# A two-block transformer kernel on one core: attention fillers reordered, forget sums moved into the key tiles

## What is computed

```
x = x + short_conv_mixer(rmsnorm(x))            # conv
x = x + swiglu(rmsnorm(x))                      # ffn1, hidden 2816
x = x + mla_mixer(rmsnorm(x))                   # mla: 8 heads, causal softmax, 1024x1024 out product
x = x + moe_swiglu(rmsnorm(x))                  # moe: 8 experts, the best 2 per token
h = x + [fox, pool](rmsnorm(x)) @ w_out         # fox: 8 heads of 64, softmax(q.k/8 + c[t] - c[s])
h = h + attention(h, mem) @ w_mem_out           # mem: 4 heads of 128 over 256 memory rows
h = h + swiglu(rmsnorm(h))                      # ffn2
```

## Time and profile before

| | us |
|---|---|
| median of 3 executions | 1348.53 |
| their lowest and highest | 1345.12, 1350.06 |
| profiled execution, own time | 1344.52 |
| its span in the trace | 1342.6 |
| granted TensorE clock (share of full) | 0.998 |

### The profile page before, as it was taken

One profiled execution on the slowest core, in us unless ns is written; L12 is line 12 of the kernel. 1 busy time (PEld: TensorE's weight loads), 2 busy tenths in 40 slices (PEclk: granted clock), 3 DMA queues, 4 the chain that ended last, 5 costly groups with the idle time before them and its releaser, 6 DMA issues.

```text
span 1342.6 us, 16314 instructions
## 1 busy us (share of the span) xinstructions
PE 1295.8 (97%) x6200; PEld 1076.8 (80%) x6200; DVE 929.4 (69%) x902; ACT 832.4 (62%) x902; POOL 39.4 (3%) x51
## 2 busy tenths in 40 slices
PE   8999999998999999999999999999999997999998
PEld 6888888887777788888888888878778776788887
DVE  4776555446759888888888888898876564645542
ACT  5645444346766778787777878777576554644431
POOL 4001000000002000000000000002010000000000
PEclk9999999999999999999999999999999999999999
DMA  9648655544218999999999999999773241455540
GB/s 332 234 152 278 213 188 184 172 124 151 106 63 332 420 359 414 357 410 357 411 351 415 356 411 354 410 365 384 258 283 126 94 158 63 166 187 182 187 157 32
DMA packets 90233, 342.20 MB, mean 255 GB/s; under 512 B 6267, under 2 KB 14160, under 8 KB 66512
## 3 DMA queue, kind: packets, MB, share of 16 engines
q1 hardware_dynamic: 87200, 330.67, 66.0%
q0 software_dynamic: 2816, 10.67, 2.3%
q10 hardware_dynamic: 160, 0.07, 0.0%
HBM read 334.05 MB, written 11.01 MB: 257 GB/s over the span
## 4 chain that ended last, share of the span: by engine, by line
PE 87%; DVE 4%; DMA 3%; ACT 3%; issue 2%; POOL 0%; ACTq 0%; SPq 0%; DVEq 0%
PE bank L1688 27%; PE bank L1690 26%; PE bank L1689 26%; DVE w_lo L367 2%; ACT w_hi L362 1%; DMA moe_slots_in<-h,row_to 1%; DMA raw<-in_moe_w_up 1%; PE bank L2026 1%; DMA raw_beside<-in_moe_w_down 1%; PE bank L1794 1%; PE bank L1821 1%; PE bank L1777 1%; DVE x L1072 1%; PE bank L2019 0%; POOL moe_slots_in L543 0%
## 5 line engine op out<-in xcount | busy, mean ns | idle before, releaser
L367 DVE TENSOR_TENSOR w_lo<-raw,w_hi 128x2048 fp32r<-128x2048 f32 (+3 forms) x246 | 549.1, 2246 | 230.3 <-ACT w_hi L362 229.2
L362 ACT ACTIVATE w_hi<-raw 128x2048 fp32r<-128x2048 f32 (+3 forms) x246 | 460.9, 1883 | 209.9 <-PE bank L1690 197.9
L1688 PE MATMUL bank<-w_hi,xT_hi 128*128 128x512 f32 (+2 forms) x672 | 256.7, 382 | 9.3 <-DVE xT_lo L1130 5.5
L1690 PE MATMUL bank<-w_hi,xT_lo 128*128 128x512 f32 (+2 forms) x672 | 253.4, 377 | 0.0
L1689 PE MATMUL bank<-w_lo,xT_hi 128*128 128x512 f32 (+2 forms) x672 | 253.3, 377 | 0.0
L1688 PE MATMUL bank<-w_hi,gT_hi 128*128 128x512 f32 x512 | 201.7, 394 | 4.7 <-DVE w_lo L367 1.9
L1690 PE MATMUL bank<-w_hi,gT_lo 128*128 128x512 f32 x512 | 200.2, 391 | 0.0
L1689 PE MATMUL bank<-w_lo,gT_hi 128*128 128x512 f32 x512 | 199.8, 390 | 0.0
L1688 PEld LDWEIGHTS bank<-w_hi,xT_hi 128*128 128x128 f32 x672 | 126.8, 189 | 34.6 <-DVE xT_lo L1130 6.8
L367 DVE TENSOR_TENSOR w_lo<-raw_beside,w_hi 128x2048 fp32r<-128x2048 f32 x64 | 145.4, 2290 | 10.0 <-ACT w_hi L362 9.9
L362 ACT ACTIVATE w_hi<-raw_beside 128x2048 fp32r<-128x2048 f32 x64 | 122.1, 1917 | 39.7 <-PE bank L1690 34.4
(11 more groups left out here) (383 smaller groups left out, 1333.3 us busy)
## 6 DMA issues: line engine op xcount, KB each, us to landing
raw<-in_moe_w_gate SPq DMA_DIRECT2D x48, 1024.0 KB, 5.0
raw<-in_moe_w_up SPq DMA_DIRECT2D x48, 1024.0 KB, 7.5
raw_beside<-in_moe_w_down SPq DMA_DIRECT2D x32, 1024.0 KB, 9.2
raw<-in_moe_w_down SPq DMA_DIRECT2D x32, 1024.0 KB, 7.6
raw<-in_w_gate_up SPq DMA_DIRECT2D x22, 1024.0 KB, 5.0
raw_beside<-in_moe_w_gate SPq DMA_DIRECT2D x16, 1024.0 KB, 5.7
raw_beside<-in_moe_w_up SPq DMA_DIRECT2D x16, 1024.0 KB, 6.5
raw<-in_ffn_w_gate SPq DMA_DIRECT2D x11, 1024.0 KB, 5.2
```

The costliest lines, as they stand in the source:

```text
L362: nc.scalar.activation(w_hi[:, slot, :n], raw_of(i, stream)[:, :n], ACT.Copy).then_inc(stream.high, 1)
L367: nc.vector.tensor_tensor(w_lo[:, slot, :n], raw_of(i, stream)[:, :n], w_hi[:, slot, :n].bitcast(F32), ALU.subtract).then_inc(stream.low, 1)
L1688: mm(dst, a_hi, b_hi, start=start, stop=False)
L1690: return mm(dst, a_lo, b_hi, start=False, stop=stop)
```

## The change

1. **Out products around the last head (mla, mem).** `out_beside` now leaves the left half of the last chunk but one to `around_last(False)`, called before `values` of the last head, and its right half to `around_last(True)`, called after it; `rest` is as before. In mla the left halves beside heads 3 and 5 and the right halves beside heads 6 and 7 stay. In mem nothing is beside head 3 any more.
2. **Fox: memory products in halves.** `memory_product(eighth)` makes 6 matmuls. Eighths 0 and 1 stay ahead of `scores(1)`; beside heads 1 to 7 stand the eighths of `BESIDE_FOX`; 14 is before the last head's values and 15 after.
3. **Fox: forget sums in the key tiles.** `fkT` gets one tile per head. The 64 rows that the other head of the pair had are cleared, and the first of them holds the head's forget sums; the same rows of `fqT` are set to -8. The selector constants and both matmuls of L2250 go. PE turns 8 tiles of 128 x 128 in place of two; DVE makes two small copies in place of one before them, and four copies of one row in place of one of 8 rows after them.
4. **Fillers of ACT and DVE.** ACT: `mixing(i)` (the pooling part) first, then `copy_turned(i)`, `value_high(i-1)`, `exps(i+1)`, and the weight split last. DVE: `mixing(i)` after `scores(i+1)`, then the split of the head before, `filled(i-1)`, then `value_low(i-1)`.
5. **More dummy matmuls:** 7 and 11 in mla before two waits for the latents, 9 in mem before the wait for the queries.
6. `moe_y` is cleared from a repeated block of 512 constants, as the constants are narrower now.

```
+BESIDE_FOX = ((), (2, 3), (4, 5), (6,), (7,), (8, 9), (10, 11), (12, 13))
...
-                for half in range(2):
-                    nc.gpsimd.memset(by_pair[FOX_DIM * (1 - half):FOX_DIM * (2 - half), :, half, :], 0.0)\
-                nc.gpsimd.memset(M["cT"][:, :], 0.0).then_inc(sem("fox_cleared"), 1)
+                for name, value in (("fqT", -(FOX_DIM ** 0.5)), ("fkT", 0.0)):
+                    by_pair = M[name].rearrange("p (k j) s -> p k j s", j=2)
+                    for half in range(2):
+                        nc.gpsimd.memset(by_pair[FOX_DIM * (1 - half):FOX_DIM * (2 - half), :, half, :], value)\
...
# ACT
-                    for stage, h in ((turn, i + 2), (copy_turned, i), (value_high, i - 1), (filled, i), (exps, i + 1)):
+                    for stage, h in ((turn, i + 2), (mixing, i), (copy_turned, i), (value_high, i - 1), (exps, i + 1),
+                                     (filled, i)):
...
-                    A_(M["fkT"][:, k, :], bank[4 + k % 2][:, S:], ACT.Copy, scale=g("g_k_fox"))\
+                    for half in range(2):
+                        ins = A_(M["fkT"][rows_, 2 * k + half, :], bank[4 + k % 2][rows_, S:], ACT.Copy,
...
# DVE
-                    for stage, h in ((probabilities, i), (turn, i + 2), (scores, i + 1), (value_low, i - 1),
-                                     (filled, i)):
+                    for stage, h in ((probabilities, i), (turn, i + 2), (scores, i + 1), (mixing, i), (filled, i - 1),
+                                     (value_low, i - 1)):
...
-                dve.wait_ge(sem("forget_sum_turned"), 1)
-                V.tensor_copy(M["cT"][:FOX_HEADS, :], bank[7][:FOX_HEADS, :S]).then_inc(sem("forget_cT"), 1)
+                dve.wait_ge(sem("fox_cleared"), 4)
+                for two in range(2):
+                    dve.wait_ge(sem("forget_sum_turned"), two + 1)
+                    for half in range(2):
+                        row = FOX_DIM * (1 - half)
+                        heads_ = M["fkT"][row:row + 1, 4 * two:4 * two + 4, :].rearrange("p (k j) s -> p k j s", j=2)
+                        V.tensor_copy(heads_[:, :, half, :],
+                                      bank[6 + two][row:row + 1, :].rearrange("p (k s) -> p k s", k=2))\
...
# PE
+                def around_last(after):
+                    if after:
+                        right(chunks - 2)
+                    else:
+                        half_of(chunks - 2, 0)
...
+                if around_last:
+                    around_last(False)
+                values(n_heads - 1)
+                if around_last:
+                    around_last(True)
...
+                keep_busy(7, 7)
                 pe.wait_ge(sem("mla_dn"), 2)
...
+                keep_busy(7, 11)
                 pe.wait_ge(sem("mla_c_low"), 2)
...
-                    for t in range(T):
-                        ins = turn_(b[:FOX_HEADS, t * P:(t + 1) * P], cs[:, 0, t, :], ident)
+                    for two in range(2):
+                        for k in range(2):
+                            for t in range(T):
+                                ins = turn_(bank[6 + two][:, (k * T + t) * P:(k * T + t + 1) * P],
+                                            sums[:, t, 2 * two + k, :], ident)
...
+                    pe.wait_ge(sem("forget_cT"), 3 + 2 * (h // 4))
                     for t, (a, keys) in enumerate(((0, P), (P, S))):
                         mm(to[:, a:a + keys], qT[:, t * P:(t + 1) * P], kT[:, :keys], start=True, stop=False)
-                        mm(to[:, a:a + keys], sel, M["cT"][:, :keys], start=False, stop=False)
...
+                keep_busy(2, 9)
                 pe.wait_ge(sem("mem_q_done"), 1)
```

More of the change, by code:

```diff
@@ L642, in ffn, with attention @@
                 w.ahead(start_of[p + "_down"] + KF // 2 - 1)
-            def attention(p, n_heads, blocks, scale, turn, value_part, filler=None, turned=0):
+            def attention(p, n_heads, blocks, scale, turn, value_part, filler=None, turned=0, mixing=lambda h: None):
                 st, p_, pT = M[p + "_st"], M[p + "_p"], M[p + "_pT"]
@@ L965, in beside @@
                         A_(M["mixed"][:, :], bank[4][:, :S], ACT.Copy).then_inc(sem("pool_mixed_copied"), 1)
+                def beside(h):
                     if h in SPLIT_BESIDE:
@@ L1106, in ffn, with attention @@
                 residual(p, w, start_of[p + "_down"] + KF // 2 - 1)
-            def attention(p, n_heads, blocks, opposite, turn, value_part, filler=None, turned=0):
+            def attention(p, n_heads, blocks, opposite, turn, value_part, filler=None, turned=0, mixing=lambda h: None):
                 st, p_ = M[p + "_st"], M[p + "_p"]
@@ L1625, in fox_value @@
                     return o[rows_, h // 2, :], bank[0][rows_, :S]
-                attention("fox", FOX_HEADS, [(0, P), (P, 3 * P)], opposite, lambda h: None, fox_value, beside)
+                attention("fox", FOX_HEADS, [(0, P), (P, 3 * P)], opposite, lambda h: None, fox_value, beside, 0, mixing)
                 w2.ahead(start_of["fox_out"])
@@ L1766, in rest @@
                     right(chunks - 1)
-                return beside, rest
+                return beside, around_last, rest
             def norm(p, src, ready):
@@ L1811, in ffn, with attention @@
                          lambda c: pe.wait_ge(sem("act_low"), before(p, "act_low") + c + 1))
-            def attention(p, n_heads, blocks, turn, score, value, filler=None):
+            def attention(p, n_heads, blocks, turn, score, value, filler=None, around_last=None):
                 def probabilities(h):
@@ L1974, in _ @@
                 CAUSAL = [(0, P), (P, 2 * P), (2 * P, 3 * P)]
-                beside, rest = out_beside("mla", W1, KD // 2, HEADS - 2, (("mla_qkT", HEADS), ("mla_ropeT", HEADS // 2)))
-                attention("mla", HEADS, CAUSAL, turn, score, value, beside)
+                beside, around_last, rest = out_beside("mla", W1, KD // 2, (HEADS - 2, HEADS - 1),
+                                                       (("mla_qkT", HEADS), ("mla_ropeT", HEADS // 2)))
+                attention("mla", HEADS, CAUSAL, turn, score, value, beside, around_last)
                 rest()
@@ L2236, in beside @@
                             .then_inc(sem("pool_mapped"), 1)
-                    if h not in (0, 4):
-                        memory_product(h if h < 4 else h - 1)
+                    for eighth in BESIDE_FOX[h]:
+                        memory_product(eighth)
                 def early_product(h):
@@ L2260, in value, with last_product @@
                     mm(b[:, P:S], v[:, 1, :], pT[:, S:], start=False, stop=True).then_inc(sem("values_in_psum"), 1)
-                attention("fox", FOX_HEADS, CAUSAL, early_product, score, value, beside)
+                def last_product(after):
+                    memory_product(15 if after else 14)
+                attention("fox", FOX_HEADS, CAUSAL, early_product, score, value, beside, last_product)
                 def turn_memory(src, name):
```

90 lines of the change are left out of this document (47 added, 43 removed).

## The result

| | before | after |
|---|---|---|
| median, us (4 executions each, side by side) | 1346.82 | 1329.78 |
| lowest and highest | 1344.16, 1350.06 | 1328.12, 1331.17 |
| ratio, 95% interval | | 0.9877 [0.9859, 0.9895] |
| profiled execution, its span | 1344.52, 1342.6 | 1329.49, 1327.3 |

The change wins 17 us by the medians and 15.3 by the two spans. Two more measurements of the same kernel gave 0.9892 [0.9872, 0.9911] and 0.9900 [0.9884, 0.9916]; over its 14 executions the median is 1330.8, against 1344.6 to 1345.5 for the kernel before in four sets of 7 to 27 executions. So 14 us is the better figure for the change.

A forecast was written before the change was run, and what follows sets the result against it. PE, busy 97% of the span, was taken as the bound. Fox 6.0, mla 2.9 and mem 1.9 summed to 10.8 us, subtracted from a median of 1348.53 to forecast 1337.7, with a range of 1332 to 1345.

The forecast's parts named there:

- The granted clock is full everywhere: Whole kernel, on PE: no stretch of lowered clock, so all durations hold at 2.4 GHz.
- the rival of a larger gain: Whole kernel: small gaps close too and matmuls behind shorter stops start faster; 13 us won, 1335.5, chance 0.10.
- Fox, 6.0 forecast: Fox's heads: selector products 4.3 and holes 2.68 won, turns 0.65 and late low parts 0.3 lost; 6.0 us.
- the new bracket: Fox, before the memory product at 1029: PE's wait for DVE to drain the banks grows to about 0.8 us.
- The 0.3 for low parts behind the split: All of fox: PE may wait before the next values where a DVE split precedes `value_low`; 0.3 us lost.
- The 0.24 taken off at head 1: Fox, behind head 1's scores: PE waits for head 0's probabilities, losing 0.24 of the 0.65 us won.
- mla, 2.9 forecast: mla's heads: waits for head 1's probabilities 0.67, head 5's values 1.31 and the last values 0.93 go; 2.9 us.
- mem, 1.9 forecast: mem's heads: waits of 1.51 and 0.93 go, a new 0.55 before the last turn comes; 1.9 us won.
- The 0.98 that a DVE operation might lose to a clearing: POOL beside DVE: a DVE operation meeting a clearing would wait for it, leaving 9.8 us won.
- Holes move instead of closing: Attention stages: the next wait of the same chain appears; 6.0 us won, 1342.5, chance 0.18.
- The rival on the other side: Fox and mla: splits ahead of `value_low` delay seven heads' next values by 2.28 each; 5.2 us slower, 1353.7, chance 0.05.
- Experts bound by their loads: Experts: loads, not PE, set their end and swallow mla's 2.9; 7.9 us won, 1340.6, chance 0.12.

The follow-up runs named there:

- no_dummies: The changed kernel without its three new groups of dummy products: 1330.27 us, ratio 0.9893 to the kernel before, against 0.9892 for the changed kernel.
- forget_only: The kernel before plus only the forget sums in the key tiles, with the narrower constants: ratio 0.9995 to the kernel before.
- around_only: The kernel before plus only mla's and mem's out products around the last head, fox's last memory quarter before its last values: ratio 0.9983 to the kernel before.
- no_order: The changed kernel with the order of ACT and DVE, and the place of mixing, as before: 1343.59 us against 1331.57 for the changed kernel.
- after: The changed kernel, whole, in its first measurement and trace: median 1329.78 us against 1346.82 for the kernel before, ratio 0.9877.
- after_again: The changed kernel unaltered, measured and traced a second time: ratio 0.9892 to the kernel before, profiled span 1333.6 us.

## Why the prediction was off

**The step that failed.** The mechanism held, hole by hole; two sizes did not. The sum of 10.8 us priced every closed hole at its bracket, where 13.5 us were found, the entry left out. And the sum was taken off a median of three executions that lay 3 to 4 us above the kernel's median over many. With both put right the forecast is 1345 - 13.5 = 1331.5, within 1 us of the 1330.8 over 14 executions. The 2.2 us of the entry in the first pair of traces are luck on top.

**The sum, 10.8 forecast.** The traces differ by 15.3. Taken apart:

- *The entry, 2.2.* Not a term of the forecast and no lasting gain, as the table shows. The sentence that failed is "The granted clock is full everywhere": the windows around 454 show 0.57. I had read the clock over 486 us, where 4 us don't show, and had not looked for what POOL's dispatches hold up. Against it stands 0.4 by which this execution was late already at 293. Without both, the change won 13.5.
- *Stops were priced at their brackets.* Each is worth 0.16 to 0.25 more. Fox closes five and opens one (PE stopped for 0.12 where it now stops for 0.78), mla closes three, mem one more than it opens: eight net, 1.3 to 2.0 us. This is the term that was mis-sized throughout; "matmuls behind a shorter stop start faster" was in the rival of a larger gain, at 0.10.
- *Fox, 6.0 forecast, 7.3 found* (8.0 less 0.7 before the scores). The turns cost what was said (0.65 against 0.64 to the DVE row at 1022.61), so did the copies (0.7 each) and the new bracket (0.78 against "about 0.8"). The 0.3 for low parts behind the split was 0.19. The 0.24 taken off at head 1 did not show as a bracket. With the stops, 0.6 to 1.0, that leaves 0 to 0.3 in gaps which I didn't resolve.
- *mla, 2.9 forecast, 3.8 found.* All three holes closed; stops give 0.5 to 0.7; 0.2 to 0.4 in small gaps is open.
- *mem, 1.9 forecast, 2.4 found.* As forecast, the wait for head 1's low part stayed: the 1.42 of the earlier trace rows before the out product is the 1.51 before head 2's values now. The old 1.51 before the last values and the 0.93 went, and the wait before the last turn was 0.29 where I put 0.55: 1.51 + 0.93 - 0.09 - 0.29 = 2.1, and a stop less.
- *The dummies, 0*: `no_dummies` agrees, as far as it can tell. *POOL, the constants, `moe_y`, 0*: nothing in the traces speaks against it. The 0.98 that a DVE operation might lose to a clearing was not lost: the eight of L1048 that ran beside the second pair of clearings, from 969.35, took 3.22, as the same eight did before.

**The median.** I took 1348.53, of three executions, and subtracted from it; the same kernel has 1344.6 to 1345.5 over 7 to 27. That put the forecast 3 to 4 us too high before any term, and it was visible: the profiled execution, 1344.52, lay 4 below. From a base of 1345 the 10.8 give 1334, inside my range, and 1330.8 is still below it.

**The rivals.** "Holes move instead of closing" at 0.18 was the right fear for parts and wrong for the whole: `forget_only` and `around_only` do exactly that. What I missed is that the parts need each other. I added them as if each had its price; the new order on ACT and DVE is what makes the other two pay, and `no_order` loses 12 of the 14. How the surplus splits between the parts the runs don't tell. The rival on the other side, splits ahead of `value_low`, cost 0.19 in all. "Experts bound by their loads" was half right: not their rate but one load, held back in SP's queue, sets the end of the first expert's up product.

## What to carry to other kernels

Price a hole by the distance from start to start against a place without one, not by its bracket alone, and search the granted clock in windows of a few us before calling it full. Reorder first, remove work second: where an engine is close behind another, removing its work alone only uncovers the next wait. On a queue that carries the weights, put a load that waits for another engine behind the weights that are needed before it.

## What the runs showed of the hardware that was not expected

**One dispatch with three lengths.** POOL's third indirect DMA took 0.95, 9.76 or 16.36 us in these traces, the last two in the changed kernel itself, while the first always took 1.02 and the second 4.11. The eight long ones all end 0.83 us behind the start of DVE's first pause in a row of weight splits. In `after` the dispatch began at 415.38 and ended at 425.14; DVE's split at 422.04 ends at 424.31, and the next has a pause before it. In `after_again` it ran from 415.99 to 432.35, and DVE's four splits ended at 431.52. DVE's rows of `after`, then of `after_again`:
```profile
422.04 2.27 DVE L365 TENSOR_TENSOR w_lo<-raw,w_hi 128x2048 fp32r<-128x2048 f32 x1
424.63 2.29 DVE L365 TENSOR_TENSOR w_lo<-raw,w_hi 128x2048 fp32r<-128x2048 f32 x1 [0.33 <-ACT w_hi L360]
```
```profile
422.64 8.88 DVE L365 TENSOR_TENSOR w_lo<-raw,w_hi 128x2048 fp32r<-128x2048 f32 x4
431.81 2.29 DVE L365 TENSOR_TENSOR w_lo<-raw_beside,w_hi 128x2048 fp32r<-128x2048 f32 x1 [0.29 <-ACT w_hi L360]
```
So the length goes with where the splits leave their first gap, and the early gap, the one of 9.76, is seen only where the half clock at 410 has slowed PE, on whose use of the weights the splits wait. The Trainium skill, page "SBUF — State Buffer", section "SBUF: two separate sides", says that DVE and GpSimd hold a shared pair of ports exclusively for a whole instruction, whichever starts first, and that a DVE operation with two inputs does so only against a GpSimd operation that reads. If a dispatch counts as reading, for its row numbers, the eight long ones agree, with their 0.83 us behind the gap. But the section "Who interferes with whom" of that page says that a `tensor_tensor`, which the split is, did not stall a DMA issued from GpSimd; if the splits are the cause here, these eight differ from it, and no run shows that they are. All 17 dispatches begin just before a split, the nine of 0.95 50 to 55 ns before it and the eight long ones 49 to 52, so a few nanoseconds may decide which one waits; that too is only argued. No run took the splits away, so the cause is argued from the coincidence in time, not shown.

**The clock falls behind short waits.** In the 17 traces stretches at half clock, most of some 3.5 us and one of 7, stand behind waits of 1.4 to 3.8 us (one of them at the start, at 11), one to four in an execution beside the one that ends each, and not always behind the same: behind the 1.50 at 410 in six of the ten traces of the changed family that have it, behind the 1.62 at 316 in two of the seven without the dummies there. Each costs half its length where PE is what is waited for, and nothing where PE had a hole ahead.
